# Expert stage of a two-block model: weight tiles become the stationary operand, and low weight tiles meet x high alone

## The reference

```python
D_MODEL = 1024; SEQ = 512; N_META = 16; N_EXPERTS = 16; EC_CAPACITY = 2
D_FF = 128 * ((8 * D_MODEL // 3 + 127) // 128)          # 2816 = 22 tiles of 128

def _expert_choice_ffn(h, norm_g, w_router, w_gate, w_up, w_down):
    b_, n_, _ = h.shape
    u = _rmsnorm(h, norm_g)
    aff = jax.nn.softmax(jnp.einsum('bnd,de->bne', u, w_router).astype(jnp.float32), axis=-1)
    cap = EC_CAPACITY * n_ // N_EXPERTS                  # 66 tokens for each expert
    g, idx = lax.top_k(jnp.swapaxes(aff, 1, 2), cap)
    xs = jax.vmap(lambda ub, ib: ub[ib])(u, idx)
    hid = (jax.nn.silu(jnp.einsum('becd,edf->becf', xs, w_gate))
           * jnp.einsum('becd,edf->becf', xs, w_up))
    y = jnp.einsum('becf,efd->becd', hid, w_down) * g[..., None].astype(h.dtype)
    return jnp.zeros_like(h).at[jnp.arange(b_)[:, None, None], idx].add(y)
```

## Time and profile before

| | us |
|---|---|
| median of three runs | 4336.51 (4333.21 to 4339.36) |
| the profiled execution: span | 4340.1 |
| PE busy in it | 4013.6 (92%) |
| weight loads (PEld) busy | 3172.6 (73%) |
| DVE busy | 3017.4 (70%) |
| ACT busy | 2295.9 (53%) |
| POOL busy | 1193.4 (27%) |

### The profile page before, as it was taken

How to read it: one execution, slowest core, us unless ns; L and a number is a source line. 1 busy time by engine, 2 the same in 40 slices (tenths; PEclk the granted TensorE clock), 3 DMA queues, 4 the chain that set the end, 5 groups by cost and what they waited for, 6 DMA issues and landing times. The chain is left out here.

```text
span 4340.1 us, 57933 instructions
## 1 busy us (share of the span) xinstructions
PE 4013.6 (92%) x21773; PEld 3172.6 (73%) x21773; DVE 3017.4 (70%) x3710; ACT 2295.9 (53%) x2928; POOL 1193.4 (27%) x555
## 2 busy tenths in 40 slices
PE   7888689999999999999699799688999999999999
PEld 6876556666666666666579777667889999978877
DVE  4364478888888888888446443443699777688885
ACT  3433257677767766776334345322237988333332
POOL 2211200010000001000222231322253555667662
PEclk9998899999999999999799899799999999999999
DMA  3212379999999999999323331323256999999995
GB/s 94 78 55 81 138 280 378 366 376 380 367 367 374 374 367 371 380 355 367 123 90 115 130 102 49 131 71 104 79 193 214 329 346 348 363 353 371 362 360 192
DMA packets 294835, 1082.17 MB, mean 249 GB/s; under 512 B 23186, under 2 KB 163730, under 8 KB 246520
## 3 DMA queue, kind: packets, MB, share of 16 engines
q1 hardware_dynamic: 254088, 936.49, 57.9%
q0 software_dynamic: 40560, 143.16, 9.0%
HBM read 1001.57 MB, written 77.97 MB: 249 GB/s over the span
## 5 line engine op out<-in xcount | busy, mean ns | idle before, releaser
L1757 ACT CAST moe_expert_high<-moe_expert_raw 128x2048 fp32r<-128x2048 f32 x570 | 973.4, 1759 | 387.4 <-DMA moe_expert_raw<-in_w_down_blocks 133.7
L1526 DVE TENSOR_TENSOR moe_expert_low<-moe_expert_raw,moe_expert_high 128x2048 fp32r<-128x2048 f32 x380 | 817.7, 2198 | 171.8 <-ACT moe_expert_high L1757 171.4
L3091 ACT CAST peer_high<-peerbuf_table_raw 128x1024 fp32r<-128x1024 f32 x256 | 255.8, 1048 | 430.0 <-PE peer_ps L3074 277.8
L679 POOL TENSOR_TENSOR branches_proj_low<-branches_proj_raw,branches_proj_high 128x2048 fp32r<-128x2048 f32 (+3 forms) x58 | 247.2, 4262 | 672.3 <-ACT branches_proj_high L659 614.2
L1644 POOL DMA_INDIRECT scratch_h<-ffn_result,ffn_y_rows x16 | 64.0, 4000 | 1232.2 <-DVE ffn_result L1796 1232.2
L1526 DVE TENSOR_TENSOR ffn_expert_low<-moe_expert_raw,moe_expert_high 128x2048 fp32r<-128x2048 f32 (+1 forms) x192 | 362.6, 1930 | 52.2 <-ACT moe_expert_high L1757 51.9
L3045 PE MATMUL peer_ps<-peerbuf_hnT_high,peer_high 128*128 128x384 f32 x1024 | 352.7, 344 | 5.2 <-ACT peer_high L3091 5.2
L2894 DVE TENSOR_TENSOR peer_low<-peerbuf_table_raw,peer_high 128x1024 fp32r<-128x1024 f32 x185 | 262.8, 1449 | 119.9 <-ACT peer_high L3091 119.7
L3046 PE MATMUL peer_ps<-peerbuf_hnT_low,peer_high 128*128 128x384 f32 x1024 | 345.2, 337 | 0.0
L1686 PE MATMUL ffn_gate_p<-moe_expert_high,ffn_x_high 128*66 128x512 f32 (+1 forms) x768 | 284.2, 377 | 1.2 <-DVE ffn_x_low L1826 1.2
L1687 PE MATMUL ffn_gate_p<-moe_expert_high,ffn_x_low 128*66 128x512 f32 (+1 forms) x768 | 283.0, 375 | 0.0
(11 more groups left out here) (551 smaller groups left out, 9379.2 us busy)
## 6 DMA issues: line engine op xcount, KB each, us to landing
moe_expert_raw<-in_w_gate_blocks SPq DMA_DIRECT2D x80, 2048.0 KB, 9.7
moe_expert_raw<-in_w_up_blocks SPq DMA_DIRECT2D x80, 2048.0 KB, 9.2
moe_expert_raw<-in_w_down_blocks SPq DMA_DIRECT2D x80, 2048.0 KB, 9.9
peerbuf_table_raw<-in_peer_down_t SPq DMA_DIRECT2D x64, 1024.0 KB, 7.7
peerbuf_table_raw<-in_peer_up_t SPq DMA_DIRECT2D x64, 1024.0 KB, 8.0
branches_proj_raw<-in_w_in SPq DMA_DIRECT2D x36, 1024.0 KB, 5.4
scratch_a<-peer_gelu SPq DMA_DIRECT2D x64, 384.0 KB, 9.2
scratch_g<-peer_spread SPq DMA_DIRECT2D x24, 1024.0 KB, 14.0
```

What stands on the lines that cost most here:

```text
L679: pool.tensor_tensor(owner.slot_of(owner.low, at), owner.slot_of(owner.raw, at), owner.slot_of(owner.high, at).bitcast(F32), ALU.subtract) ...
L1526: return engine.tensor_tensor(self.half_of(self.low, q, h), self.half_of(self.raw, q, h), self.half_of(self.high, q, h).bitcast(F32), ALU. ...
L1757: act.copy(half_of(high, q, h), half_of(raw, q, h)).then_inc(high_done, 1)
L3091: act.copy(high[:, q % 2, cols], raw[:, q % PR_RAW, cols]).then_inc(high_done, 1)
```

## The change

Chunks are now 384 columns wide (three tiles of 128; seven chunks and one of 128), the ring has four blocks instead of three, and an expert has 24 blocks. In all three products the stationary operand is now a 128 x 128 tile of the weights and the moving operand holds tokens. For a high weight tile it is the pair [x high | x low], 132 columns, in one matmul (`x_pair`, `t_pair`); for a low weight tile it is x high alone, 66 columns. The two halves of the pair land side by side in PSUM, so they must be added: ACT copies one half out, DVE adds the other (steps "sum"; `take_down` and `sum_down` for the result). The result of gate and up has hidden columns on the partitions, as the down product wants it, so `turn` goes; instead the expert's result has to be transposed (`turn_y`, 8 matmuls). The PE program of the first expert is written out ahead of the loop over the other fifteen.

```diff
-FF_CHUNK = 512
+FF_CHUNK = 384
-FF_RING = 3
+FF_RING = 4
 FF_AHEAD = 2
+PAIR = 2 * CAP
+PAIR_ROW = 192
+T_RING = 3
...
-                        hi, lo, out = block_of(high, q), block_of(low, q), psum[:CAP, s, 0:width]
+                        hi, lo = block_of(high, q), block_of(low, q)
+                        if c >= 2 or not first:
+                            pe.wait_ge(summed, e * FF_N + c - 1)
                         high_in(q)
-                        for k in range(KD):
-                            pe.matmul(out, x_high[:, k, 0:CAP], hi[:, k, :], start=(k == 0), stop=False)
-                            pe.matmul(out, x_low[:, k, 0:CAP], hi[:, k, :], start=False, stop=False)
+                        for f in range(n):
+                            for k in range(KD):
+                                pe.matmul(psum[:, s, f * PAIR:(f + 1) * PAIR], hi[:, k, f * P:(f + 1) * P],
+                                          x_pair[:, k, 0:PAIR], start=(f == 0 and k == 0), stop=False)
                         low_in(q)
-                        for k in range(KD):
-                            last = pe.matmul(out, x_high[:, k, 0:CAP], lo[:, k, :], start=False, stop=(k == KD - 1))
+                        for f in range(n):
+                            for k in range(KD):
+                                last = pe.matmul(psum[:, s, f * PAIR:f * PAIR + CAP], lo[:, k, f * P:(f + 1) * P],
+                                                 x_pair[:, k, 0:CAP], start=False, stop=(f == n - 1 and k == KD - 1))
                         last.then_inc(block_used, 1)
...
-                        for t, cols in parts:
-                            pe.matmul(down_p[:CAP, cols], t_high[:, s, t, 0:CAP], hi[:, t, cols],
-                                      start=(c == 0 and t == 0), stop=False)
-                            pe.matmul(down_p[:CAP, cols], t_low[:, s, t, 0:CAP], hi[:, t, cols], start=False, stop=False)
+                        for t in range(n):
+                            for k in range(KD):
+                                pe.matmul(down_p[:, k // 3, k % 3 * PAIR:(k % 3 + 1) * PAIR], hi[:, t, k * P:(k + 1) * P],
+                                          t_pair[:, c % T_RING, t, 0:PAIR], start=(c == 0 and t == 0 and k % 3 == 0),
+                                          stop=False)
                         low_in(q)
...
                     for c in range(FF_N):
-                        pe.wait_ge(hidden_done, e * FF_N + c + 1)
-                        columns("gate", c, gate_p)
-                        columns("up", c, up_p)
-                        if c >= 1:
-                            turn(c - 1)
+                        columns("gate", c, gate_p, gate_summed)
+                        columns("up", c, up_p, up_summed)
+                        for a in range(2):
+                            if not first and at[("up", c)] == y_at[a]:
+                                turn_y(e - 1, a)
...
+                            if step == "sum":
                                 act.wait_ge(block_used, used(e, "gate", c))
+                                if c >= 2 or not first:
+                                    act.wait_ge(hidden_done, e * FF_N + c - 1)
+                                act.copy(gate[:, s, 0:n, :], sums(gate_p, c, 1)).then_inc(part_out, 1)
+                                act.wait_ge(block_used, used(e, "up", c))
+                                act.copy(up[:, s, 0:n, :], sums(up_p, c, 1)).then_inc(part_out, 1)
```

More of the change, by code:

```diff
@@ L1554, in expert_ffn @@
         ring.block_of, ring.half_of, ring.raw, ring.high, ring.low, ring.raw_in, ring.high_done, ring.low_done)
+    tail = FF_N - 1
+    y_at = (at[("up", 2)], at[("up", 3)])
+    steps_at = {q: [] for q in range(FF_NB)}
+    for c in range(FF_N):
+        i = at[("up", c)]
+        summed, joined, parted = (i + 3, i + 4, i + 5) if c < tail else (FF_NB - 2, FF_NB - 1, FF_NB - 1)
+        steps_at[summed].append(("sum", c))
+        steps_at[joined].append(("join", c))
+        steps_at[parted].append(("part", c))
+    steps_at[FF_NB - 2].append(("x", 0))
+    steps_at[FF_NB - 1].append(("x", 1))
+    rank = {"part": 0, "join": 1, "sum": 2, "x": 3}
+    for q, steps in steps_at.items():
+        steps.sort(key=lambda s: (s[1] if s[0] != "x" else FF_N, rank[s[0]] if s[1] != tail else -rank[s[0]]))
     with Stage(nc, "ffn") as st:
-        low.append(st.sb("expert_low2", [P, KD * FF_CHUNK], F32R))
+        for q in range(FF_AHEAD, FF_RING):
+            low.append(st.sb(f"expert_low{q}", [P, KD * FF_CHUNK], F32R))
         x_raw = st.sb("x_raw", [CAP, D])
@@ L1592, in x_turned_part @@
         def x_turned_part():
[L1593 to L1604, removed]
-                    if c >= 1:
[L1606 to L1612, removed]
+            return turn_p[:, 0:KD // 2 * CAP].rearrange("p (k c) -> p k c", c=CAP)
@@ L1716, in down @@
-                        low_in(q)
-                        for t, cols in parts:
-                            last = pe.matmul(down_p[:CAP, cols], t_high[:, s, t, 0:CAP], lo[:, t, cols], start=False,
-                                             stop=(c == FF_N - 1 and t == width // P - 1))
+                        for t in range(n):
[3 more added lines that the diff above has]
+                                          stop=False)
@@ new lines, in down @@
+                        low_in(q)
+                        for t in range(n):
+                            for k in range(KD):
+                                last = pe.matmul(down_p[:, k // 3, k % 3 * PAIR:k % 3 * PAIR + CAP],
+                                                 lo[:, t, k * P:(k + 1) * P], t_pair[:, c % T_RING, t, 0:CAP],
+                                                 start=False, stop=(c == tail and t == n - 1 and
+                                                                    (k % 3 == 2 or k == KD - 1)))
@@ L1739, in _, with take_down, take_y, take_x @@
                     down(FF_N - 1)
+                turn_x(0, 0)
+                pe.wait_ge(x_low_done, 1)
+                turn_x(0, 1)
+                expert(0, first=True)
+                with pe.Fori(1, EXPERTS) as e:
+                    expert(e)
+                pe.wait_ge(x_low_done, 2 * EXPERTS + 2)
+                turn_y(EXPERTS - 1, 0)
+                turn_y(EXPERTS - 1, 1)
             @block.scalar
             def _(act):
-                act.sem_inc(result_out, 2)
-                def take_result(e):
-                    act.wait_ge(block_used, used(e, "down", FF_N - 1))
+                def take_down(e):
+                    act.wait_ge(block_used, used(e, "down", tail))
+                    for part in range(2):
+                        act.copy(y_part(part), y_sums(part, 1)).then_inc(y_part_out, 1)
+                def take_y(e):
+                    act.wait_ge(y_turned, 2 * e + 1)
                     act.wait_ge(result_free, e + 1)
-                    act.activation(result[:, 0:512], down_p[:CAP, 0:512], ACT.Copy,
+                    act.activation(result[:, 0:512], turn_p[:CAP, :], ACT.Copy,
                                    scale=slot_gate[:, bass.ds(e, 1)]).then_inc(result_out, 1)
+                def take_x(e, a):
+                    act.wait_ge(x_turned, 2 * e + a + 3)
+                    act.copy(x_part(a, 0), x_turned_part()).then_inc(x_high_done, 1)
                 def expert(e, first=False):
@@ L1764, in expert @@
                                 act.wait_ge(hidden_done, e * FF_N + c + 1)
[L1765 to L1767 removed]
+                                if c >= T_RING:
+                                    act.wait_ge(block_used, used(e, "down", c - T_RING))
+                                act.copy(t_part(c, 0), hidden[:, s, 0:n, :]).then_inc(t_high_done, 1)
+                            else:
@@ L1829, in _ @@
+                        if q == y_at[1] + 4 and not first:
+                            take_y(e - 1)
                 take_x(0, 0)
```

178 lines of the change are left out of this document (92 added, 86 removed).

## The result

The changed kernel takes 6510.3 us (median of 4 runs, 6506.2 to 6515.7), the kernel before 4334.9 us (4 runs, 4329.2 to 4339.4): a ratio of 1.501 with an interval of 1.498 to 1.504. It is 2175 us longer.

A forecast was written before the change was run, and what follows sets the result against it. PE and the weight transfers were both taken as the bound, within 3%. Sum: 4340.1 - 1519.2 (old expert stage) + 3645 (new) + 8 (tail) = 6474 us profiled, so 6470 us; range 5300 to 6600 us.

The forecast's parts named there:

- The pace: Expert stage, PE: weight loads set the time between matmul starts, 0.112 us at full clock, 0.2125 us at half.
- the lower clock: Expert stage: PE stays at clock 0.50, falling back if lifted; 3645 us for 16 experts; chance 77%.
- Two of its reasons: Expert stage: it starts at 0.50 with nothing dense to lift it, and only 99 columns on average stream behind each load.
- the first rival: Expert stage: dense matmuls run at full clock all through, 120.0 us an expert, 4740 us in all; chance 10%.
- An expert 227.8 us: PE per expert at the lower clock: 1056 matmuls at 0.2125 us, 224.4, plus 16 transposes, 3.4.
- The tail: End of expert stage: two sums, eight transposes and a second ACT and DVE round; 8 us at half clock.
- next to nothing for PE: Kernel before, expert stage: ACT waits 346 us for arriving weights and hardly at all for PE.
- ACT at 81 and DVE at 92 us an expert: Expert stage: casts, subtractions and small steps on ACT and DVE, all hidden behind 120 or 228 us of PE.
- wait of PE for the sums: PE's new waits for the sums of chunk c-2, five blocks behind the summed block: cost nothing.
- The side of a gain: Rival: the load is not the floor; stage falls to DVE and transfers, 4300 us in all; chance 5%.

The follow-up runs named there:

- The kernel at 4742.9: Changed kernel with low tiles meeting 132 columns, PE's program without a loop, and 20 extra 512-column matmuls at the first expert only: 4742.9 us, ratio 1.094.
- the one at 6468.0: Changed kernel with PE's program written out for all sixteen experts instead of a loop over the last fifteen, nothing else: 6468.0 us, ratio 1.492.
- the third experiment: Changed kernel with 20 extra matmuls of 512 columns at the start of each expert, result unread: 6522.8 us, ratio 1.504.
- half the load: Changed kernel with 64 instead of 128 columns in 952 of an expert's 1056 stationary tiles: 4431.5 us; with the next x gathered before the store, 4319.4 us.

## Why the prediction was right

**The sum by its terms.** The 2175 us divide into three by the medians of four kernels:

| part | from | us |
|---|---|---|
| load floor at full clock | 4742.9 - 4335.4 | 408 |
| lower clock | 6468.0 - 4742.9 | 1725 |
| jump of the loop | 6510.3 - 6468.0 | 42 |

The kernel at 4742.9 differs from the one at 6468.0 by the low tiles' 132 columns and the twenty matmuls too; the first cost nothing (6516.1 beside 6510.3), the second some 7 us.

**The pace.** Forecast 0.112 us at full clock and 0.2125 at the lower one, for 132 and 66 columns alike; measured 0.112 and 0.213. Reading the pace from starts of another line's 128 x 128 loads carried over, also from its float32 pass to float32r tiles. The Trainium skill, TensorE: Matmul & The Clock Gate, section Back-to-back issue gap, gives about 81 ns for a sustained pair of load and matmul with 128 columns; the runs show 112 ns at 2.4 GHz, and the measurement decides.

**The clock.** The forecast gave 77% to the lower clock, from one stretch in which loads were busy all the time and nothing rose. The changed kernel shows 0.50 for 3.7 ms with PE stopping only at the jumps. Two of its reasons were tried. Lifting the clock at an expert's entry does not last. With more columns behind the same loads the stage runs at full clock: with 240 it rises by itself, with 132 everywhere it needs a lift and then holds.

The evidence was thin, and it covered only half of what was said. The same line L2478 had run at full clock 7 us before the two runs of the earlier trace rows began. The clock then fell around a stretch in which PE worked only 1.95 of 3.40 us:
```profile
2711.77 2.79 PE L2478 MATMUL dil_mixed<-dilbuf_qkv 128*128 128x64 f32 x24
```
```profile
2713.70:2717.10 3.40, 1.95 (x16) 1.57 (x15) 0.59 (x3) 3.35 (x5) 0.00 (x0) 1.00 0.00 0
2717.10:2720.50 3.40, 2.52 (x13) 2.52 (x13) 0.00 (x0) 1.90 (x4) 0.00 (x0) 0.51 0.22 82
```
So the stretch showed 10 us in which such a stream did not bring the clock back. That it would also lose a clock once it had it, which the forecast said too, stood in no row; the third experiment shows it. And there was luck in it: with the low tiles' other 66 columns, one lift and no jumps the program takes the first rival's time.

The rule behind the first rival, that dense back-to-back matmuls stay at full speed (the same page, section Loop structure matters more than you think), does not hold here: in the third experiment PE worked 219.5 of 222 us at 0.50. The rival's number was good: full clock all through was priced at 4740 us, and the kernel that has it takes 4743.

**The terms left out or off.** "An expert 227.8 us" was 227.6 without the jump and 230.6 with it. The forecast counted matmuls and transposes and nothing between two experts; the kernel before shows no such pause, so no row of before bounded it. Against the forecast of 6474 us the profiled execution took 6504.4, 30 us more. The 14 jumps add 42 of these; the experts' own work came out 4 us shorter, and everything outside the stage had been put 7 us too long. The tail is part of that: it was put at 8 us, but from the end of the last product to the start of the last scatter-add it grew by 4.3 us (from 1.7 to 6.0). The medians lie 40.3 us apart, since this profiled execution is 6 us under its median where the one before was 3.6 over. So part of the forecast's closeness is errors that cancel.

One reading was loose: ACT's casts waited "next to nothing for PE". They waited 41 us in the stage (22.8 for a down block to be given back, 18.1 for a gate block) beside 346 for transfers. It changes no term.

**What was costed at nothing.** Chunks and ring: 0.9 us with an interval across zero. ACT at 81 and DVE at 92 us an expert: 72.5 and 87.0 in one period, behind 230 of PE, as said. The forecast for ACT was high because a cast of 1536 elements takes 1.36 us, not 1.48. The profile has no wait of PE for the sums.

**The side of a gain.** The rival was put at 4300 us for the case of a load that costs nothing; with half the load the program takes 4319 once x is gathered early. The figure stands. Its condition, that the full load costs nothing, was false.

## What to carry to other kernels

Before making the wide operand stationary, count weight loads, not columns: in this kernel's float32 and float32r streams a 128-column load costs 0.112 us at 2.4 GHz, and anything from 64 to 240 moving columns rides free on it. Here a 128 x 512 piece of weights cost three passes of 0.23 us while it moved, 0.69 us, and costs eight loads of 0.112 us now that it stands, 0.90. Then ask, from a stretch of the trace that looks like the new stream, whether it holds TensorE's clock: a stage can be dense on PE and still run at half speed, and that cost four times what the floor did.

## What the runs showed that was not expected

- **The jump back of a long loop.** PE stands idle for 2.4 to 3.8 us at each jump, in a body of some 1070 matmuls with their loads. The kernel before with chunks of 384 has a loop of the same kind with 546 matmuls, and there PE waits for nothing after the stage's first matmul. Why the longer body pauses was not tried; unrolling removes the pause. Where the clock is high, a pause there can drop it as well.
- **The issue of the scatter-add on POOL.** The median of 16 is 1.51 us in the changed kernel, 4.88 before, and 25.4 with half tiles. DVE's share of the stage does not rank them: it is 84% in the last two alike. What differs is the moment: in the changed kernel DVE stands still when the issue starts, in the kernel before it is at work then, and with half tiles it goes on without a gap for some 25 us. The Trainium skill, SBUF — State Buffer, section Who interferes with whom, states that GpSimd can be starved of the port by which it writes a DMA's descriptors while DVE is in a mode with two ports, but also that `tensor_tensor` has no such mode and did not stall a DMA. DVE's work here is nearly all TENSOR_TENSOR, so by the page's account the descriptors should not have been held up. DVE's load was not varied alone; the cause stays open.
- **The load follows the clock.** 128 columns take 190 ns at 2.4 GHz and 333 at 1.2, so a stream bound by loads doubles in time like one bound by columns (0.112 to 0.213 us). At either clock the columns below the load's time save next to nothing.
